# HGRN stage of a hybrid encoder layer: a level's product on 64 columns, a masked copy in place of multiply and add, and other places for the level steps

## What is computed

```python
def hgrn_step(s_state, inp):
    q, k, v, lf = inp
    causal = jnp.tril(jnp.ones((length, length), dtype=bool))[:, :, None]
    a = jnp.cumsum(lf, axis=2)
    rel = jnp.where(causal, a[:, :, :, None, :] - a[:, :, None, :, :], -jnp.inf)
    scores = jnp.einsum('bhtk,bhsk,bhtsk->bhts', q, k, jnp.exp(rel))
    o = jnp.einsum('bhtk,bhkv->bhtv', q * jnp.exp(a), s_state) + jnp.einsum('bhts,bhsv->bhtv', scores, v)
    a_end = a[:, :, -1:]
    s_new = jnp.exp(a_end[:, :, 0])[..., None] * s_state + jnp.einsum('bhsk,bhsv->bhkv', k * jnp.exp(a_end - a), v)
    return s_new, o
```

## Time and profile before

| | us |
|---|---|
| median of 3 runs | 2456.49 (2455.03 to 2457.44) |
| the profiled execution: its time | 2456.35 |
| the profiled execution: span of the trace | 2454.5 |
| PE (TensorE matmuls) busy | 2369.7, 97% |
| DVE (VectorE) busy | 1120.1, 46% |
| ACT (ScalarE) busy | 747.0, 30% |
| POOL (GpSimd) busy | 81.7, 3% |
| HGRN stage, four heads of 100.5 each | about 1604 to 2006 |

### The profile page before, as it was taken

How to read it: one execution, slowest core, us unless ns; L and a number is a source line. 1 busy time by engine, 2 the same in 40 slices (tenths; PEclk the granted TensorE clock), 3 DMA queues, 4 the chain that set the end, 5 groups by cost and what they waited for, 6 DMA issues and landing times.

```text
span 2454.5 us, 46387 instructions
## 1 busy us (share of the span) xinstructions
PE 2369.7 (97%) x19389; PEld 2293.1 (93%) x19389; DVE 1120.1 (46%) x1661; ACT 747.0 (30%) x1113; POOL 81.7 (3%) x111
## 2 busy tenths in 40 slices
PE   6999999999999999999999999998999989999998
PEld 5999999999999999989989999898998979999998
DVE  5342323234242324735536536356666475445454
ACT  5222222222222222323233233232333333234443
POOL 0000000000000000000000000002012020000000
PEclk9999999999999999999999999999999999999999
DMA  4213212131312222112112121131121234444465
GB/s 164 88 69 109 91 68 108 58 118 56 119 62 99 90 85 94 50 46 88 57 45 99 45 87 58 45 137 69 51 96 46 98 112 165 158 143 142 149 205 189
DMA packets 54540, 236.74 MB, mean 96 GB/s; under 512 B 7858, under 2 KB 13156, under 8 KB 31972
## 3 DMA queue, kind: packets, MB, share of 16 engines
q1 hardware_dynamic: 54452, 235.40, 27.2%
HBM read 209.92 MB, written 25.45 MB: 96 GB/s over the span
## 4 chain that ended last, share of the span: by engine, by line
PE 83%; DVE 7%; issue 4%; ACT 3%; DMA 2%; SPq 0%; DVEq 0%; ACTq 0%; POOL 0%; POOLq 0%
PE acc L728 62%; PE acc L1180 5%; PE branch L918 2%; PE branch L1180 2%; PE branch L956 2%; DVE w_lo L1570 1%; ACT w_hi L1227 1%; DVE scratch L2062 1%; PE branch L911 1%; DVE scratch L2061 1%; DVE scratch L2024 1%; DMA scratch<-in_x_all 1%; DMA w_raw<-in_w_stream 1%; PE branch L828 0%; DVE scratch L1796 0%
## 5 line engine op out<-in xcount | busy, mean ns | idle before, releaser
L728 PE MATMUL acc<-act_hi,w_hi 128*128 128x288 f32 (+2 forms) x4416 | 1339.7, 303 | 9.5 <-DVE w_lo L1570 7.6
L728 PE MATMUL acc<-act_lo,w_hi 128*128 128x288 f32 (+2 forms) x4416 | 1309.4, 297 | 0.0
L728 PE MATMUL acc<-act_hi,w_lo 128*128 128x288 f32 (+2 forms) x4416 | 1308.2, 296 | 0.0
L728 PEld LDWEIGHTS acc<-act_hi,w_hi 128*128 128x128 f32 x4416 | 834.1, 189 | 23.4 <-DVE w_lo L1570 9.0
L728 PEld LDWEIGHTS acc<-act_lo,w_hi 128*128 128x128 f32 x4416 | 834.0, 189 | 0.7
L728 PEld LDWEIGHTS acc<-act_hi,w_lo 128*128 128x128 f32 x4416 | 833.8, 189 | 0.0
L1570 DVE TENSOR_TENSOR w_lo<-w_raw,w_hi 128x2048 fp32r<-128x2048 f32 x169 | 388.5, 2299 | 779.9 <-ACT w_hi L1227 776.7
L1227 ACT ACTIVATE w_hi<-w_raw 128x2048 fp32r<-128x2048 f32 x169 | 323.6, 1915 | 187.4 <-PE branch L1180 127.1
L1180 PE MATMUL acc<-act_hi,w_hi 128*128 128x288 f32 x384 | 114.0, 297 | 3.9 <-DVE act_lo L2125 3.9
L1180 PE MATMUL acc<-act_hi,w_lo 128*128 128x288 f32 x384 | 113.9, 297 | 1.5 <-issue 1.5
L1180 PE MATMUL acc<-act_lo,w_hi 128*128 128x288 f32 x384 | 114.2, 298 | 0.0
(11 more groups left out here) (394 smaller groups left out, 1980.6 us busy)
## 6 DMA issues: line engine op xcount, KB each, us to landing
w_raw<-in_w_stream SPq DMA_DIRECT2D x170, 1024.0 KB, 4.9
gate_logits<-gate_out SPq DMA_DIRECT2D x48, 288.0 KB, 2.2
scratch<-gate_logits SPq DMA_DIRECT2D x48, 288.0 KB, 3.2
scratch<-in_x_all SPq DMA_DIRECT2D x9, 512.0 KB, 6.3
branch_rows<-branch_out SPq DMA_DIRECT2D x16, 288.0 KB, 2.1
scratch<-in_x_all SPq DMA_DIRECT2D x3, 1024.0 KB, 10.1
out_y_prompt<-scratch SPq DMA_DIRECT2D x6, 512.0 KB, 2.7
scratch<-branch_rows SPq DMA_DIRECT2D x1, 2304.0 KB, 9.5
```

Source lines behind the costliest of these rows:

```text
L728: last = mm(acc[s][:, at:at + hi - lo], a[:, s, w], b[:, k, lo:hi], start=(k == 0 and a is whi and b is xh), stop=(k == KT - 1 and a is wlo))
```

## The change

1. A level's product moves 64 columns of a chunk, those of the second blocks, and its stationary side is always 128 columns wide, for the 80-token chunk too. All levels write to `brb`, even levels at column 0, odd ones at 512.
2. VectorE clears `PS` at the head's start, and each level writes its columns into it with `copy_predicated` under a mask. The products into `PT` and all additions on GpSimd are gone.
3. The product of a token with itself runs first, then the levels.
4. Places on TensorE, in blocks after the start of N(2) (the list now begins there): 8 same token, 10 `turn_k`, 12, 15, 20 levels 0 to 2, 22 `turn_v`, 23, 26, 29, 34 levels 3 to 6, 36 `updates`, 40 `outputs`, 50 `turn_o`. Counted in the same way the old ones were 30 and 31 for the transposes, 35, 37, 39, 42, 44, 46, 48, 50 for the eight products, 52, 55 and 62.
5. The orders on ScalarE and VectorE are written anew around that.

```diff
-        "levels": np.concatenate([level_mask(lv) for lv in range(LEVELS)] + [s == t], 1),
+        "levels": np.concatenate([level_mask(lv)[:, seconds(lv)] for lv in range(LEVELS)] + [s == t], 1),
...
                 def level_pairs(lv):
-                    bank = br[lv % 2]
-                    pe.wait_ge(*vt.after(i, f"scaled{lv}" if lv < LEVELS else "k"))
-                    if lv >= 2:
-                        pe.wait_ge(*vt.after(i, f"masked{lv - 2}"))
...
+                    w = 1 << lv
+                    pe.wait_ge(*vt.after(i, f"scaled{lv}"))
+                    pe.wait_ge(*vt.after(i, f"masked{lv - 2 if lv >= 2 else LEVELS}"))
+                    for c in range(1 if lv == 6 else 0, NCH):
+                        q = QK[lv % 2][:, START[c]:START[c] + P]
+                        o = 512 * (lv % 2) + 64 * c
+                        last = mm(brb[:, o:o + 64], q, q.rearrange("p (n two w) -> p n two w", two=2, w=w)[:, :, 1, :], start=True, stop=True)
+                    pt.done(last, f"pairs{lv}")
+
+                def same_token():
+                    pe.wait_ge(*vt.after(i, "k"))
+                    pe.wait_ge(evac_done, N(1) + 1)
                     for c in range(NCH):
                         tok = slice(START[c], START[c] + LEN[c])
-                        if lv == 6 and c == 0:
-                            continue
-                        a, b = (QK[lv % 2], QK[lv % 2]) if lv < LEVELS else (bk, bq)
-                        last = mm(bank[0:LEN[c], P * c:P * c + LEN[c]], a[:, tok], b[:, tok], start=True, stop=True)
-                    pt.done(last, f"pairs{lv}")
+                        last = mm(brb[0:LEN[c], P * c:P * c + LEN[c]], bk[:, tok], bq[:, tok], start=True, stop=True)
+                    pt.done(last, f"pairs{LEVELS}")
...
-                for j in range(3):
+                for j in range(2):
                     product(N(j), cols=QUERY_COLS if j == 1 else FULL_COLS)
-                products([N(3), N(4), N(5)],
-                         [(14, turn_k), (15, turn_v)]
-                         + [(at, lambda lv=lv: level_pairs(lv)) for lv, at in enumerate((19, 21, 23, 26, 28, 30, 32, 34))]
-                         + [(36, updates), (39, outputs), (46, turn_o)])
+                products([N(2), N(3), N(4), N(5)],
+                         [(8, same_token), (10, turn_k)]
+                         + [(at, lambda lv=lv: level_pairs(lv)) for lv, at in enumerate((12, 15, 20))]
+                         + [(22, turn_v)]
+                         + [(at, lambda lv=lv: level_pairs(lv)) for lv, at in ((3, 23), (4, 26), (5, 29), (6, 34))]
+                         + [(36, updates), (40, outputs), (50, turn_o)],
+                         cols=[FULL_COLS, EVEN_COLS, EVEN_COLS, EVEN_COLS])
...
@@ ScalarE
+                level_exp(0)
+                rows_of(khtok, "k_turned", "k_rows")
+                level_exp(1)
                 in_order(N(2), bv)
                 split_hi(N(4))
...
+                level_exp(2)
+                level_exp(3)
+                rows_of(vbtok, "v_turned", "v_rows")
+                level_exp(4)
+                level_exp(5)
                 src = source(N(3))
                 f(split2(bz[:, 0:KEPT]), src, ACT.Copy)
                 f(split2(bez[:, 0:KEPT]), src, ACT.Exp, scale=-1.0).then_inc(evac_done, 1)
                 split_hi(N(5))
...
+                level_exp(6)
                 act.wait_ge(*G.after(i, "outputs"))
...
@@ VectorE
+                v.memset(PS[:, :, :], 0.0)
...
                 V.done(v.memset(qhat[:, NS:C0], 0.0), "meta_from_zero")
-                split_lo(N(4))
...
                 def level_masked(lv):
...
-                        v.tensor_tensor(dst[0:C0, 0, 0:C0], bank[0:C0, 0:C0], mk[0:C0, 0:C0], ALU.mult)
-                    V.done(v.tensor_tensor(dst[:, 1:5, :], bank[:, P:5 * P].rearrange("p (c n) -> p c n", c=4),
-                                           mk.unsqueeze(1).to_broadcast([P, 4, P]), ALU.mult), f"masked{lv}")
+                    V.done(v.copy_predicated(PS[:, first:NCH, :].rearrange("p c (n two w) -> p c n two w", two=2, w=w)[:, :, :, 1, :],
+                                             chosen(masks[:, mo:mo + 64].rearrange("p (n w) -> p n w", w=w), [P, n, 64 // w, w]),
+                                             brb[:, o:o + 64 * n].rearrange("p (c n w) -> p c n w", c=n, w=w)), f"masked{lv}")
...
                 level_scaled(0)
                 level_args(1)
+                same_token()
                 level_scaled(1)
-                for lv in range(LEVELS + 1):
-                    if lv + 2 < LEVELS:
-                        level_args(lv + 2)
+                level_args(2)
+                split_lo(N(4))
+                for lv in range(LEVELS):
                     level_masked(lv)
+                    if lv == 4:
+                        split_lo(N(5))
                     if lv + 2 < LEVELS:
                         level_scaled(lv + 2)
-                    if lv == 0:
-                        split_lo(N(5))
-                    elif lv == LEVELS - 1:
-                        split_lo(N(6))
+                    if lv + 3 < LEVELS:
+                        level_args(lv + 3)
...
@@ GpSimd: the additions L2281 and L2282 and their loop are removed
```

More of the change, by code:

```diff
@@ L218 @@
         logit logit0 soft_inv softmax bound rest f1 f2 k f3 f log_copy log_sums end_args args0 ends khat
-        meta_from_zero scaled0 args1 scaled1 args2 masked0 scaled2 args3 masked1 scaled3 args4 masked2
-        scaled4 args5 masked3 scaled5 args6 masked4 scaled6 masked5 no_pairs6 masked6 masked7 state1
+        meta_from_zero scaled0 args1 masked7 scaled1 args2 masked0
+        scaled2 args3 masked1 scaled3 args4 masked2 scaled4 args5 masked3 scaled5 args6 masked4 scaled6
+        masked5 masked6 state1
         state2 state3 state4 states z1 z2 gate o_unit y""",
     "hgrn_scalar": """
-        soft log_f decay_exp end_exp exp0 k_rows v_rows exp1 exp2 exp3 exp4 exp5 exp6 o_sum0 o_sum1
+        soft log_f decay_exp end_exp exp0 k_rows exp1 exp2 exp3 v_rows exp4 exp5 exp6 o_sum0 o_sum1
         o_sum2 o_sum3 o_sum4 o_log o_rstd""",
     "hgrn_tensor": """
-        k_turned v_turned pairs0 pairs1 pairs2 pairs3 pairs4 pairs5 pairs6 pairs7 updates outputs
+        pairs7 k_turned pairs0 pairs1 pairs2 v_turned pairs3 pairs4 pairs5 pairs6 updates outputs
         o_turned""",
-    "hgrn_pool": """
-        add1 add2 add3 add4 add5 add6 summed""",
     "norm_rows_tensor": """
@@ L521, in build @@
         C_ = {k: steps(k) for k in ("rwkv_vector", "rwkv_scalar", "rwkv_tensor", "rwkv_pool")}
-        B_ = {k: steps(k) for k in ("hgrn_vector", "hgrn_scalar", "hgrn_tensor", "hgrn_pool")}
+        B_ = {k: steps(k) for k in ("hgrn_vector", "hgrn_scalar", "hgrn_tensor")}
         A2 = {k: steps(k) for k in ("norm_rows_tensor", "norm_rows_scalar")}
@@ L1475, in _ @@
                 split_hi(N(5))
-                for lv in range(1, LEVELS):
-                    act.wait_ge(*V.after(i, f"args{lv}"))
-                    S.done(f(EE, EE, ACT.Exp), f"exp{lv}")
-                act.wait_ge(gates_out[0], i * 16 + 16 * (NH_A * 2 + NP_C * 2))
-                plain(N(4), gbuf[0][:, :])
-                split_hi(N(6))
+                level_exp(6)
                 act.wait_ge(*G.after(i, "outputs"))
@@ L2070, in level_masked @@
[L2070 to L2078 removed]
+                    own(f"masked{lv - 1 if lv else LEVELS}")
@@ new lines, in same_token @@
+                def same_token():
+                    dve.wait_ge(*G.after(i, f"pairs{LEVELS}"))
+                    dve.sem_inc(masks_begun, 1)
+                    mo = CONST_AT["levels"][0] + 64 * LEVELS
+                    mk = masks[:, mo:mo + P]
+                    v.copy_predicated(PS[0:C0, 0, 0:C0], mk[0:C0, 0:C0].bitcast(mybir.dt.uint16), brb[0:C0, 0:C0])
+                    V.done(v.copy_predicated(PS[:, 1:5, :], chosen(mk, [P, 4, P]), brb[:, P:5 * P].rearrange("p (c n) -> p c n", c=4)), f"masked{LEVELS}")
@@ L2115, in _ @@
                 V.done(last, "o_unit")
+                split_lo(N(6))
                 dve.wait_ge(*G.after(i, "o_turned"))
@@ L2273, in _ @@
                 Q.done(g.tensor_tensor(DDT[:, :, :], each, each, ALU.mult), "unit_blocks")
-            G, V, Sc, Q = (B_[k] for k in ("hgrn_tensor", "hgrn_vector", "hgrn_scalar", "hgrn_pool"))
-            with looped(pool, 0, NH_B) as i:
-                for lv in range(1, LEVELS + 1):
-                    pool.wait_ge(*V.after(i, f"masked{lv}"))
-                    if lv > 1:
-                        pool.wait_ge(*Q.after(i, f"add{lv - 1}"))
-                    g.tensor_tensor(PS[0:C0, 0, 0:C0], PS[0:C0, 0, 0:C0], PT[lv % 2][0:C0, 0, 0:C0], ALU.add)
-                    Q.done(g.tensor_tensor(PS[:, 1:5, :], PS[:, 1:5, :], PT[lv % 2][:, 1:5, :], ALU.add), f"add{lv}" if lv < LEVELS else "summed")
             def row_scales(p, cols):
```

55 lines of the change are left out of this document (25 added, 30 removed).

## The result

| | before | after |
|---|---|---|
| median, us | 2456.28 (2455.03 to 2457.44, 4 runs) | 2481.84 (2479.66 to 2484.43, 4 runs) |
| profiled execution, us | 2456.35 | 2482.49 |
| span of its trace, us | 2454.5 | 2480.5 |
| mean granted clock of TensorE | 0.992 | 0.984 |
| four heads of HGRN, us | 402.0 | about 426.5 |

The change makes the kernel slower: the ratio after to before is 1.0105, interval 1.0087 to 1.0122. The forecast was slower too, but at 2470, and 2481.8 lies above the upper end of the range, 2477. A head is counted from the wait for N(2)'s remainder to the same wait in the next head: 100.5 us before; after, 109.0 in the first head and 105.9 in the next two. The fourth ends where the merge begins and is 5.3 us longer than before.

The account below looks back on a forecast made before the run. TensorE, busy 97% of the span, was taken as the bound. Added 2.1 + 12.8 + 18.8 + 9.5 = 43.2 us, less 28.9 removed, is +14.3 on 2456.35: 2470; own range 2463 to 2476, 8-in-10 range 2455 to 2477.

Parts of the forecast that it names:

- Removed, 28.9 us: HGRN stage: 14 level_scaled waits and turn_o's wait go, 22.5 us idle, plus 3.1 start-up and 3.3 halved clock.
- The price of a level, +2.1: Level products on TensorE: each of six levels costs 0.09 us more, over four heads +2.1 us.
- the upper bound, 1.08: Ten passes of a level: 1.08 us if every pass takes 0.111 us; the lower bound was 0.029 us a pass.
- passes are priced by moved columns: Rival, level products: moved columns set a pass's price, giving 2456 or down to 2448; chance 0.10 no change, 0.05 faster.
- The first new wait, 3.2 us a head: Level 2's product, four blocks into N(3), waits for its scaling behind N(4)'s remainder and level 0's copy; 12.8 us in all.
- the masked copy is slow: Rival, VectorE ahead of level 2: copy takes two steps per column, 0.42 us more a head, 2472; within the 0.67 for slower.
- The second new wait, 4.7 us: Level 6's product, two blocks into N(4), waits for its scaling behind N(5)'s high part and remainder; 18.8 us over four heads.
- The clock behind these waits, +9.5: TensorE's clock falls to 0.50 behind seven of the eight new waits, costing 1.35 us each, +9.5 us.
- clock holds: Rival, TensorE behind the new waits: the clock does not fall, 9.5 us are not paid, 2461, no change; chance 0.10.

Follow-up runs that it names:

- Experiment 4: Changed kernel with ScalarE and VectorE orders rewritten so that level 2's and level 6's scalings go ahead of the weight-tile remainders, removing both new waits: 2427.92 us, ratio 0.9886.
- experiments 7 and 8: Both on the changed kernel reordered to remove both new waits: 7 with 64 stationary columns in place of 128, 2424.15 us; 8 with all 128 columns moved, 2429.51 us.
- Experiment 1: Changed kernel with unused products on TensorE ahead of the level 2 and level 6 waits, to keep it busy there: 2461.58 us, ratio 1.0022.
- experiment 2: Changed kernel with exponential 6 ahead of the output gate's copies and level 6's scaling ahead of N(5)'s remainder, removing only level 6's wait: 2453.48 us, ratio 0.999.
- experiment 3: Changed kernel with exponentials 2 and 3, level 0's copy and level 2's scaling moved earlier, removing only level 2's wait: 2458.41 us, ratio 1.0008.
- experiment 10: Changed kernel with level 2 two blocks later and level 6 three blocks later on TensorE, neighbours moved alike: 2458.41 us (2450.75 to 2464.40), ratio 1.0006.
- experiment 5: Kernel before with 64 moved columns, masked copy into PS and no GpSimd additions, but old places and orders: 2436.25 us, ratio 0.9916.

## Why the prediction was wrong, point by point

The direction and both mechanisms held; the time did not. The profiled executions differ by 26.1 us, of which the four heads are 24.5. The other 1.6 lie outside the stage: the stage begins 2.3 us later, in the part that the change doesn't touch, behind a slow stretch at 43.5 us that before's trace lacks, and what follows it is 0.9 shorter; I count both as scatter.

- **Removed, 28.9 us: right to 1 us.** Experiment 4, in which all of the change is in and neither new wait, takes 351.4 us from the first wait to the merge against 379.3: 27.9 less. The price of the passes (1.0) and the small waits of the first head (0.9) stand in that, so some 29.8 went.
- **The price of a level, +2.1: half.** Ten passes take 1.03 us, where I took the upper bound, 1.08. (The 0.11 us for a load of 128 columns that I read from the earlier trace rows was a slip: 50 ns for 48 columns make 0.13.) That is +1.0 in place of +2.1. The choice between the bounds was right: experiments 7 and 8 show the stationary side setting the price, so the rival "passes are priced by moved columns" is out.
- **The first new wait, 3.2 us a head: 3.5.** The place and queue are as forecast; the masked copy takes 0.66 us to the next start and not 0.42. The rival "the masked copy is slow" had 0.42 us more a head; 0.24 came, 1 us in all.
- **The second new wait, 4.7 us: 4.7.**
- **The clock behind these waits, +9.5: this is the step that failed.** I had taken seven stretches and held that one costs between 0 and 1.7 us, 1.35 each. The trace has eight, at 2.3 on average. Three are 3.4 us long and five 6.8, 44.4 us together, of which 3.3 lie inside the waits themselves. At 0.50 the product steps in 0.240 us, at 1.00 in 0.131, so 41.1 us of work lost 41.1 x (1 - 0.131/0.240) = 18.7. That is 9.2 us more than forecast. I had read one slow stretch, 3.4 us long, and taken its price as the upper bound for all. In the changed kernel those behind level 6 are the long ones: 6.1 us of work at 0.50 costs 2.8 us each, the short ones 1.5. Experiment 1 measures the whole term by itself, at 20.3 us by the medians and 18.9 between its trace and the changed kernel's from the first wait to the merge; experiments 2 and 3 gained 9.5 and 9.4 beyond the waits that they took away.

The length of the wait alone does not set the length of the stretch. Behind 4.6 us of idle it is 6.8 us in all eight cases (the changed kernel and experiment 3). Behind 3.3 us it is 3.4 in four cases and 6.8 in four (the changed kernel and experiment 2), and behind 2.2 us it is 3.4 once and 6.8 three times (experiment 10). What decides between the two lengths stays open.

The longer stretch stood in the trace of before, in a place that I had not read: the merge begins behind a wait of 3.88 us. Its window, before, and under it the one behind the same wait of 3.88 us in the changed kernel:

```profile
2010.80:2017.60 6.80, 5.26 (x24) 5.15 (x23) 3.96 (x6) 2.68 (x6) 0.00 (x0) 0.50 0.93 302
2036.90:2040.20 3.30, 3.18 (x13) 3.21 (x14) 3.30 (x6) 3.30 (x7) 0.00 (x0) 0.50 0.87 248
```

The first row has 5.26 us of work at 0.50, or 2.4 us lost. With that as the price of the four waits of 4.7 us, and 1.35 for the other three, the term would have been 13.6 and the time 2475, inside the range though still low. What the row could have given is the upper bound: up to 3.1 us for a stretch of 6.8 us that is all work.

- **Small waits in the first head, not forecast.** The transposes of the keys waited 0.7 us there and the same-token copy let level 0 wait 0.3.

In sum, in us: 14.3 forecast, + 9.2 clock, + 1.2 first wait, + 0.1 second, + 1.0 small waits, - 1.1 passes makes 24.7, against 24.5 in the four heads. With the 0.9 more that went it is 23.8; the sum is good to about 1 us.

The rival "clock holds" would have given 2461; experiment 1, where it holds although the same time passes, gave 2461.6. The range ended at 2477 because its upper end took every stretch at 1.65, the price of the only one I had priced. Its own terms do not even reach 2477: 2470.6 with 1.7 for the slow copy and seven stretches at 1.65 is 2474, with eight 2476.

## What to carry to other kernels

Moving a stage earlier on the engine that bounds the kernel pays only if the chain that feeds it ends by then: list the queue of the feeding engine at the new place, above all the long instructions ahead of it (here 2.2 us of `split_lo` behind 1.9 of `split_hi`), and either move the feeder ahead of them or the consumer behind them. Price an idle gap on TensorE as the gap and the slow stretch behind it: here 32.9 us of waits drew 18.7 us of clock. Take the upper bound of that price from the longest slow stretch in the whole trace and not from the first one found: here equal waits drew stretches of 3.4 and of 6.8 us. Before halving one side of a matmul, see which side sets its step: with new weights for each pass 64 moved columns more cost nothing, and 64 stationary ones fewer gained 0.2 us a level.

## What the runs showed of the hardware

- Idle of about 1.75 us brought TensorE's clock to 0.50 in two cases of four (experiment 10), idle of 1.9 to 2.1 us in two of four (the kernel before), idle of 2.2 us in four of four, and the times of the kernel with these waits scatter by 14 us in ten runs. The changed kernel's waits of 3.3 and 4.6 us brought it down each time, eight of eight. Waits of 1.1 us for the remainder brought none.
- The slow stretch in the stage was either 3.4 or 6.8 us long. Equal waits drew both: 3.3 us of idle the short one four times and the long one four times, 3.88 us ahead of the merge the long one before and the short one after.
- Ten float32 passes with fresh weights take 1.03 us for 128 stationary columns with 64 or with 128 moved, and 0.72 for 64 by 64. From load to load a pass does halve, from 0.113 to 0.058 us; with the steps into and out of it the whole level falls from 1.16 to 0.95 us.
- A masked copy out of PSUM, 320 columns with 16-bit masks, takes 0.87 us on VectorE where single columns or pairs alternate (levels 0 and 1) and 0.50 at levels 2 to 5; a multiplication of 512 columns took 0.68.
- `level_scaled` beside a GpSimd addition took 1.84 us and alone takes 0.46. The Trainium skill, "SBUF — State Buffer", section "SBUF: two separate sides", says that a VectorE instruction with two SBUF inputs and a GpSimd instruction that reads SBUF lock each other out of a port pair for the whole instruction; the earlier trace rows agree: the instruction of 1.84 us ends 0.3 us behind the addition. So does experiment 5, where without the additions, and with the shorter copy, 16.5 of 18.3 us of waits are gone.
